# Strassen's seven products for the up projections of the last three feed-forwards

## The reference

```python
def rmsnorm_2(x, g):
    y = x32 * lax.rsqrt(jnp.mean(x32 * x32, axis=-1, keepdims=True) + RMS_EPS)
    return (y * g).astype(x.dtype)

def swiglu(h, w_gate, w_up, w_down):
    return (jax.nn.silu(h @ w_gate) * (h @ w_up)) @ w_down

x = x + MACARON_WEIGHT * swiglu(rmsnorm_2(x, norm_g[i, 0]), ...)   # weight 0.5
```

## Time and profile before

| | |
|---|---|
| median of 3 runs | 2765.05 us (2763.44 to 2765.18) |
| span of the profiled execution (first to last instruction) | 2761.3 us |
| PE busy | 2733.8 us, 99% |
| DVE / ACT / POOL busy | 1166.5 / 1039.8 / 1111.9 us (42 / 38 / 40%) |
| chain that ended last | PE 88%, issue 7%, POOL 2%, DVE 2% |

### The profile page before, as it was taken

How to read it: one execution, slowest core, us unless ns; L and a number is a source line. 1 busy time by engine, 2 the same in 40 slices (tenths; PEclk the granted TensorE clock), 3 DMA queues, 4 the chain that set the end, 5 groups by cost and what they waited for, 6 DMA issues and landing times.

```text
span 2761.3 us, 35493 instructions
## 1 busy us (share of the span) xinstructions
PE 2733.8 (99%) x12420; PEld 2172.9 (79%) x12420; DVE 1166.5 (42%) x1908; ACT 1039.8 (38%) x1594; POOL 1111.9 (40%) x475
## 2 busy tenths in 40 slices
PE   9999999999999999999999999999999999999999
PEld 7777777888888888857888888888888754888887
DVE  5886534755534224256883222122221366422211
ACT  4555533444333223343233222232222466422222
POOL 3234433444444443523224444544445410444443
PEclk9999999999999999999999999999999999999999
DMA  5333322333333232322113323333333210323332
GB/s 168 121 98 117 106 78 63 92 99 99 99 106 99 91 99 91 114 76 88 54 46 107 99 91 104 106 95 99 99 98 105 87 39 9 107 91 99 98 102 89
DMA packets 80030, 257.29 MB, mean 93 GB/s; under 512 B 11577, under 2 KB 16697, under 8 KB 79691
## 3 DMA queue, kind: packets, MB, share of 16 engines
q1 hardware_dynamic: 73424, 244.74, 28.5%
q10 hardware_dynamic: 6522, 11.43, 1.3%
HBM read 249.98 MB, written 6.03 MB: 93 GB/s over the span
## 4 chain that ended last, share of the span: by engine, by line
PE 88%; issue 7%; POOL 2%; DVE 2%; ACT 1%; DMA 0%; POOLq 0%; DVEq 0%; ACTq 0%
PE ps L823 25%; PE ps L824 25%; PE ps L825 25%; POOL wlo L772 2%; PE ps L1463 1%; PE ps L1432 1%; PE ps L1445 1%; PE ps L1213 1%; PE ps L1242 1%; PE ps L1436 1%; PE ps L1192 1%; PE ps L1261 1%; PE ps L1119 1%; PE ps L1129 1%; PE ps L1052 0%
## 5 line engine op out<-in xcount | busy, mean ns | idle before, releaser
L772 POOL TENSOR_TENSOR wlo<-raw,whi 128x1024 fp32r<-128x1024 f32 x449 | 1098.2, 2449 | 1605.1 <-ACT whi L1545 1580.3
L823 PE MATMUL ps<-lin_hi,whi 128*128 128x512 f32 x2200 | 864.0, 393 | 0.0
L825 PE MATMUL ps<-lin_hi,wlo 128*128 128x512 f32 x2200 | 856.3, 389 | 0.0
L824 PE MATMUL ps<-lin_lo,whi 128*128 128x512 f32 x2200 | 856.1, 389 | 0.0
L1545 ACT ACTIVATE whi<-raw 128x1024 fp32r<-128x1024 f32 x452 | 473.1, 1052 | 517.7 <-PE ps L825 444.7
L823 PEld LDWEIGHTS ps<-lin_hi,whi 128*128 128x128 f32 x2200 | 413.0, 188 | 92.3 <-issue 6.1
L824 PEld LDWEIGHTS ps<-lin_lo,whi 128*128 128x128 f32 x2200 | 413.0, 188 | 88.4 <-issue 3.1
L825 PEld LDWEIGHTS ps<-lin_hi,wlo 128*128 128x128 f32 x2200 | 412.9, 188 | 85.7
L823 PE MATMUL ps<-act_hi,whi 128*128 128x512 f32 x858 | 334.0, 389 | 0.0
L825 PE MATMUL ps<-act_hi,wlo 128*128 128x512 f32 x858 | 333.8, 389 | 0.0
L824 PE MATMUL ps<-act_lo,whi 128*128 128x512 f32 x858 | 333.8, 389 | 0.0
(11 more groups left out here) (420 smaller groups left out, 2769.7 us busy)
## 6 DMA issues: line engine op xcount, KB each, us to landing
raw<-in_packs SPq DMA_DIRECT2D x456, 512.0 KB, 3.5
table<-bias_scratch ACTq DMA_DIRECT2D x12, 256.0 KB, 3.2
bias_scratch<-biasrow ACTq DMA_DIRECT2D x16, 160.0 KB
x<-in_x_t SPq DMA_DIRECT2D x4, 512.0 KB, 8.4
out_t<-x SPq DMA_DIRECT2D x14, 128.0 KB, 1.9
bias_scratch<-biasrow ACTq DMA_DIRECT2D x4, 320.0 KB
mem<-in_mem_t ACTq DMA_DIRECT2D x1, 1024.0 KB, 7.8
pool_count<-in_pool_count ACTq DMA_DIRECT2D x1, 1024.0 KB, 4.8
```

Of the source, the lines that this page charges most:

```text
L772: pool.tensor_tensor(wlo[:, n % 4, :], raw[:, n % 2, :], whi[:, n % 4, :].bitcast(F32), ALU.subtract).then_inc(low_split, 1)
L823: pe.matmul(target, wh, hi[:, k, :], start=(chunk0 + at == 0), stop=False)
L824: pe.matmul(target, wh, lo[:, k, :], start=False, stop=False)
L825: mm = pe.matmul(target, wl, hi[:, k, :], start=False, stop=(chunk0 + at == total - 1))
```

## The change

The weights of a pair (gate and up tile) and two chunks of 128 inputs that lie 512 inputs apart form a 2x2 block matrix, and so do the two data chunks with their two halves of 256 tokens. The plain way takes eight block products. The change takes seven, of 4 chunks each, with sums of blocks on both sides. Per pair and with the three matmuls of the two-part float32 that is 7 x 4 x 3 = 84 matmuls of 128x256 in place of 2 x 8 x 3 = 48 of 128x512.

- **Weights.** `load_pair` brings a pair (two packs) into `raw_pair`. DVE makes four more [128, 512] blocks from them (`pair_sums`). The seven blocks fill slots 0 to 2 (1024 wide) and 3 (512 wide), split as before by ACT and POOL.
- **Data.** `fold` takes the place of `residual`'s chunk: DVE makes the block sums of two chunks, ACT and DVE split them into `folds`, seven blocks each.
- **Results.** A pair takes four banks (`4 * (p % 2)` and on). ACT copies single products out of PSUM (`copy_term`) before PE adds on to the same bank; DVE adds bank and copy for each quarter (`take_quarter`), scales (`scale_part`), multiplies and splits.
- **Groups.** The pairs go in groups of 8, 8 and 6; after each group its part of the down projection is done and added to `x` (8 packs each of 8, 8 and 6 chunks).

```diff
+GROUPS = (8, 8, 6)
+PRODUCTS = (
+    (0, 0, 0, 0, True), (0, 1, 1, 4, True), (1, 0, 2, 1, True), (1, 1, 0, 5, False),
+    (2, 0, 1, 6, False), (2, 1, 3, 2, True), (3, 0, 0, 3, False),
+)   # slot, half, bank, fold, begins
...
+        def seven_pair(name, g, p, i, s=None, banks_after=None):      # PE
...
+            def product(k, steps):
+                slot, half, bank, fold, begins = PRODUCTS[k]
+                for c in steps:
...
+                    pe.matmul(target, wh, folds[c][:, fold, 0, :], start=begins and c == 0, stop=False, skip_group_check=True)
+                    pe.matmul(target, wh, folds[c][:, fold, 1, :], start=False, stop=False, skip_group_check=True)
+                    mm = pe.matmul(target, wl, folds[c][:, fold, 0, :], start=False, stop=c == 3, skip_group_check=True)
...
+            if pair >= 2:
+                pe.wait_ge(quarter_steps, value(i, 12, 6 * (pair - 1) - 1))
+            for k, (slot, half, bank, fold, begins) in enumerate(PRODUCTS):
+                if half == 0 and (s is None or slot == 3):
+                    pe.wait_ge(low_split, value(i, 8, n + slot + 1))
...
+                if k in (3, 4, 6):
+                    pe.wait_ge(terms_copied, value(i, 8, 4 * pair + (1, 2, 3)[(3, 4, 6).index(k)]))
...
+        def copy_term(name, g, p, i, k):                              # ACT
...
+        def seven_window(name, g, p, i, n, s=None, next_packs=None):  # ACT
+            split_pair(name, g, p, 3, i)
+            if p:
+                silu(name, g, p - 1, i, n)
+            copy_term(name, g, p, i, 0)
+            if p:
+                hidden_split(name, g, p - 1, i, n)
+            copy_term(name, g, p, i, 1)
+            for slot in range(3):
+                if next_packs is None:
+                    split_pair(name, g, p + 1, slot, i)
+                else:
+                    split_high(next_packs + slot)
...
+                if slot < 2:
+                    copy_term(name, g, p, i, 2 + slot)
...
+        def pair_sums(name, g, p, i, k):                              # DVE
...
+                dve.tensor_tensor(block[2], block[1], block[0], ALU.subtract).then_inc(sums_made, 1)
+                dve.tensor_tensor(block[7], block[0], block[5], ALU.add).then_inc(sums_made, 1)
...
+        def take_quarter(name, g, p, i, k, done=None):
...
+            dve.tensor_tensor(target, ps[:, 4 * (p % 2) + bank, FIRST_HALF], terms[p % 2][:, term, :], ALU.add).then_inc(quarter_steps, 1)
...
+        def scale_part(name, g, p, i, part):
+            take_quarter(name, g, p, i, 2 + part)
...
+            dve.tensor_tensor(target[:, :], target[:, :], rstd[:, :], ALU.mult).then_inc(quarter_steps, 1)
...
+        def seven_window(name, g, p, i, n, more=True, s=None):        # DVE
+            if p:
+                scale_part(name, g, p - 1, i, 0)
+            if more:
+                pair_sums(name, g, p + 1, i, 0)
+            if p:
+                scale_part(name, g, p - 1, i, 1)
+            if more:
+                pair_sums(name, g, p + 1, i, 1)
+            if p:
+                make_hidden(name, g, p - 1, i, n)
+                low_hidden(name, g, p - 1, i, n)
+            take_quarter(name, g, p, i, 0, n)
...
+            take_quarter(name, g, p, i, 1)
```

More of the change, by code:

```diff
@@ L736, in _, with load_plain, load_pair @@
                 load_waves()
-        with sp.Fori(hyena // 4 - 4, mla // 4 - 8) as i:
-            for n in range(32, 36):
-                load(n, i)
+        def load_plain(n, wait, at):
+            sp.wait_ge(low_split, wait)
+            sp.dma_start(raw[:, n % 2, :], A["packs"][at]).then_inc(raw_arrived[n % 2], 16)
+        def load_pair(name, g, p, i, wait):
+            for part, to in enumerate((slice(1, 4, 2), slice(0, 6, 5))):
+                at = DRAM_BASE[f"{name}_up"] + 2 * (sum(GROUPS[:g]) + p) + part
+                src = A["packs"][bass.ds(value(i, 4, at), 1), :, :].rearrange("a p (s c) -> p (a s) c", s=2) if i is not None else \
+                    A["packs"][at].rearrange("p (s c) -> p s c", s=2)
+                if part == 0:
+                    sp.wait_ge(low_split, wait)
+                sp.dma_start(raw_pair[p % 2][:, to, :], src).then_inc(pair_arrived[p % 2], 16)
@@ new lines, in seven @@
+        def seven(name, after, last_order):
+            for g, pairs in enumerate(GROUPS):
+                base, down = PACK_BASE[f"{name}_up{g}"], PACK_BASE[f"{name}_down{g}"]
+                with sp.Fori(0, pairs // 2 - 1) as i:
+                    for p in (2, 3):
+                        load_pair(name, g, p, i, value(i, 8, base + 4 * (p - 1)))
+                order = last_order if g == 2 else range(DC)
+                for d in range(DC):
+                    load_plain(down + d, base if d < 2 else down + d - 1, DRAM_BASE[f"{name}_down"] + 3 * order[d] + g)
+                    if d == 1 and (g < 2 or after):
+                        for p in range(2):
+                            load_pair(name if g < 2 else after, g + 1 if g < 2 else 0, p, None, base + 4 * (pairs - 1 + p))
@@ L780, in _ @@
             split_low(n, None)
-        with pool.Fori(1, times) as i:
-            for n in range(4):
-                split_low(n, i)
-        for n in range(queries - rest, queries):
-            split_low(n, None)
+        split_packs(4, PACK_BASE["ffn1_up0"] - 4)
+        seven("ffn1")
+        seven("ffn2")
+        split_packs(PACK_BASE["mla_down"], queries - PACK_BASE["mla_down"])
         for n in range(queries, queries + 4):
@@ L1333, in query_sums @@
+        seven("ffn1", 5, 2 * FC, "pool_hyena_out")
+        seven("ffn2", 6, 3 * FC, "ffn1_down2")
         def query_sums():
@@ new lines, in seven @@
+        def seven(n, name, s, after):
+            for g, pairs in enumerate(GROUPS):
+                seven_window(name, g, 0, None, n, s=s if g == 0 else None)
+                with dve.Fori(0, pairs // 2 - 1) as i:
+                    for p in (1, 2):
+                        seven_window(name, g, p, i, n)
+                last = pairs - 1
+                seven_window(name, g, last, None, n, more=False)
+                scale_part(name, g, last, None, 0)
+                scale_part(name, g, last, None, 1)
+                make_hidden(name, g, last, None, n)
+                low_hidden(name, g, last, None, n)
+                phase = f"{name}_down{g}"
+                if g == 2 and after is None:
+                    last_residual(phase, s + 1, factor=0.5)
+                elif g == 2 and after not in SEVENS:
+                    residual(phase, s + 1, factor=0.5)
+                elif g == 2:
+                    residual_to_pairs(phase, s + 1, 0.5, after)
+                else:
+                    for j in range(DC):
+                        take(phase, j, j, 0.5)
+                        if j in (4, 5):
+                            pair_sums(name, g + 1, 0, None, j - 4)
@@ L2807, in _ @@
         latent_out_low(7)
[L2808 to L2809 removed]
+        residual_to_pairs("mla_out", 8, 1.0, "ffn3")
+        seven(4, "ffn3", 8, None)
     ctx.close()
```

443 lines of the change are left out of this document (346 added, 97 removed).

## The result

The changed kernel takes 3092.89 us (median of 4 runs, 3086.11 to 3097.55) against 2765.11 us beside it on the same chip (4 runs, 2763.44 to 2765.62): ratio 1.1186, 95% interval 1.1171 to 1.1202. It is slower; the forecast was 3035 with a range of 2930 to 3130. (The profiled execution took 3094.05 us for a span of 3092.2, so 1.9 us lie around the span, not 3.7; that is why the spans miss the forecast by 61 us and the medians by 58.)

A forecast was written before the change was run, and what follows sets the result against it. PE bound the kernel before; with the change, waits through DVE, ACT and the port shared with POOL would set the pairs. 196.6 + 44 + 24 + 6 - 0.6 = +270 us gave 3035 us, range 2930 to 3130.

The forecast's parts named there:

- PE's work: Matmuls of a pair: 84 x 0.120 = 10.08 us in place of 10.88, over 66 pairs -52.9 us.
- The circle and the port: Up projections: product 5 waits for ACT's copy behind DVE, whose SBUF port POOL shares; full pair 14.96 us, +196.6 us.
- The clock: After PE's waits in each pair: loss at 1.2 GHz 0.96 us, mostly absorbed, so nothing added to the sum.
- E: The end of PE's work on the pair before, from which the chain was laid out; PE resumes at E + 10.64.
- twice that: Pairs' low clock: twice the +55 us if the low level lasts twice as long.
- The rival that priced the clock at +55: Full and last pairs: 57 x 0.96 us lost at low clock, giving 3090 us; 10% for above 3100.
- Group ends: The down part waits for the last low half, POOL's splits in the chain: 6 x 4.5 + 3 x 5.8 = +44 us.
- Loads: 0: A pair's two transfers of 3.5 us, asked for 13 us before they are needed, stay hidden: 0.
- Folds: Block sums of the data: DVE's and POOL's work beside the packs, between 0 and 44 us, taken as +24.
- kernel end: Last tile: its second half shrinks to 18 matmuls while DVE's 8.8 us for the first half stays: +6 us.
- The chain without the port: Rival for the pairs: POOL never meets DVE, pairs take 11.19 us, kernel 2780 us; 12%.
- PE as the bound: Rival for the pairs: the circle closes within 5.76 us, PE stays the bound, kernel 2717 us; 6%.

The follow-up runs named there:

- e2: Changed kernel with POOL computing the low part of only 8 columns of each slot of the up weights: 2844.9 us, ratio 1.0289.
- e5: Changed kernel with ACT doing each group's last Silu and high half before the splits of down packs 2 and 3: 3035.6 us, ratio 1.0985.
- e6: Changed kernel with DVE making most low parts of the up weights, DVE and ACT reordered without the circle, and e5's group ends: 2787.1 us, ratio 1.0084.
- e9: e6 with DVE also making low parts in the folds, block sums earlier before ffn2 and ffn3, and the norm's reciprocal later: 2778.6 us, ratio 1.0053.
- e10: Changed kernel with ACT's first three copies of a pair ahead of the high half of the pair before: 3029.9 us, ratio 1.0960.

## Why the forecast was right, and where it was off

**PE's work: right.** Inside a product matmuls of 256 columns start 0.12 us apart, as in the earlier trace rows.

**The circle and the port: right, in mechanism and size.** 14.96 us a full pair and 11.8 a last one were laid out from rows of before. With the clock held up they measured 14.89 and 11.81. The reading that carried it was that DVE with two inputs in SBUF and POOL's split exclude each other and serve the one that waits; e2 switches that off and finds the other layout, 11.15 for 11.19. It is also the rule of the Trainium skill ("SBUF — State Buffer", Who interferes with whom), and the traces agree with it: the scaling took 2.10 us on average beside POOL's splits and 0.69 in e2. (POOL's pauses before were 6.1 us of every 10.9 by the earlier trace rows, not 5.8; nothing hung on it.)

**The clock: the step that failed.** "Most of a later E would be absorbed, since POOL's splits then end before it" put its price at nothing. The pair at 2311 shows both parts: PE resumed at E + 9.4 in place of 10.64, so 1.2 us were absorbed, but its three last products took 6.0 us (2321.0 to 2327.0) in place of 4.32, so 1.65 were lost, not 0.96. The 0.96 came from a window of the earlier trace rows that ended inside the low stretch. The next window of the kernel before shows the rest:

```profile
226.00:228.00 2.00, 2.00 (x13) 2.00 (x12) 1.96 (x7) 0.00 (x0) 2.00 (x1) 0.63 0.56 143
```

That is 1.5 us more at 1.2 GHz, 3.4 in place of 1.9, so 1.7 us lost each time, the case that the rival named as "twice that". Most of it was absorbed indeed, but not all: on average full pairs took 15.56 for 14.96 and last ones 11.04 for 11.8: +28.8 - 6.8 = +22 us in the sum, up projections +218.9 for +196.6. The rival that priced the clock at +55 named 3090; that this met the measured time is luck, since the pairs gave 22 of its 55 and group ends and folds the rest. The Trainium skill ("TensorE: Matmul & The Clock Gate", Part 1), which I had set aside, would have the clock fall at many of the waits; 322 us at 1.2 GHz agree.

**Group ends: about the right wait, by the wrong cause.** +44 forecast, 48.5 us of waits measured. But I had laid out POOL's splits in DVE's way, and e5 shows that most of it was ACT's queue: 7.8 of 8.4 us go when Silu no longer stands behind splits that wait for a transfer. "Loads: 0" was true of the pairs and not of the down packs. With the low clock behind each wait six of the ends cost 8.4 us, not 4.5: +23 us.

**Folds, third group ends and kernel end.** Forecast 17.4 + 24 + 6 - 0.6 = 47 us, measured 61.6 (330.9 in all less 218.9 and 50.4). The fold before ffn2 with its group end is 67.63 - 42.72 = 24.9 of it. DVE's gains and sums were blocked there as said. A part that the forecast had no term for is the 17.6 us that PE waited for POOL's low parts in the three first pairs after the folds. The end's 5.6 us of wait is the +6.

The three differences, 22 + 23 + 15, make the 60 us by which the span missed. All three have one sign; the range held them since it reached 95 us above the forecast, for the clock.

**The rivals.** The chain without the port is e2: 2845, not 2780, with its group ends (36.3 us of PE's waits) and folds unmended. What comes nearest to PE as the bound is e6, built by hand: 10.57 us a pair, where PE needs 10.08. In e9 its 57 distances sum to 586.6, so the up projections take 677.3 us (nine first pairs at 10.08) against 718.1 before: 41 us of the 53 that the seven products promise do arrive, and group ends, folds and the end take 55 back.

## What to carry to other kernels

Fewer matmuls pay only if the operations that make them possible find free time on the engines that prepare the operands: here eight DVE instructions a pair with two SBUF inputs and POOL's splits together wanted 12.9 us of one port in a 10.1 us pair. Lay out the chain from the end of one iteration to the point where PE waits, with each queue's order: it gave the pair to 1%, and named the copy that closes the circle. Follow what else stands in the same queue too: moving one copy moved the circle on to the next, and moving three moved it on to the splits. Where waits of PE of some 4 us are forecast, price the low clock behind them over its whole stretch (look at the window after the one in which it begins). And where a queue holds an instruction behind one that waits for a transfer, put it ahead.

## What the runs showed that I had not expected

- The clock was still 1.00 while PE stood (2317 to 2321) and fell to 0.50 when it had been busy again for some 1.5 us, so the windows over the wait and over its cost are different ones.
- A DVE instruction of 0.69 us took up to 2.90 us between two of POOL's splits (a block sum of e10 at 2815.81), and a gain with one SBUF input and a column of scales was blocked as well, 2.57 us beside POOL and 0.49 without.
